# A hybrid attention and 32-expert layer: router on unscaled rows, first and last experts in another order, down weights in 8 KB pieces, activations transposed by every eighth column

## What is computed

```python
x = x + concat([y_a, y_b]) @ w_o                  # x1
h = rms_norm(x, g_ffn)                            # h2
logits = (h @ w_router + b_router)                # 512 x 32
top_vals, top_idx = top_k(logits, 4);  gates = softmax(top_vals)
# for each expert e, for the rows that chose it (at most 128 at a time):
gu  = xb @ w_gu[e] + b_gu[e]                      # 1024 -> 2048
glu = minimum(gu[:, :1024], 7.0);  lin = clip(gu[:, 1024:], -7.0, 7.0)
act = glu * sigmoid(1.702 * glu) * (lin + 1.0)
y   = (act @ w_down[e] + b_down[e]) * gate        # 1024 -> 1024
out = x + sum of the y of each row's four experts
```

## Time and profile before

| | us |
|---|---|
| median of 3 runs | 1613.7 (1611.57 to 1614.81) |
| the profiled execution | 1612.47 |
| its span, first to last instruction | 1610.7 |
| TensorE busy | 1479.8 (92%) |
| VectorE busy | 1313.3 (82%) |
| ScalarE busy | 1107.4 (69%) |
| GpSimd busy | 298.1 (19%) |
| mean granted TensorE clock | 0.955 of full |

### The profile page before, as it was taken

One profiled execution on the slowest core, in us unless ns is written; L12 is line 12 of the kernel. 1 busy time (PEld: TensorE's weight loads), 2 busy tenths in 40 slices (PEclk: granted clock), 3 DMA queues, 4 the chain that ended last, 5 costly groups with the idle time before them and its releaser, 6 DMA issues.

```text
span 1610.7 us, 18681 instructions
## 1 busy us (share of the span) xinstructions
PE 1479.8 (92%) x7095; PEld 1218.0 (76%) x7098; DVE 1313.3 (82%) x1251; ACT 1107.4 (69%) x1198; POOL 298.1 (19%) x161
## 2 busy tenths in 40 slices
PE   6888758997589999999999999999999999999993
PEld 5776646776467888888888888888888888888882
DVE  4668856544668999999999999999999999999991
ACT  5543354443557787778878878887787788877771
POOL 1634301001201111121112111211121121111101
PEclk9999957998799999999999999999999999999997
DMA  6312011107589999999999999999999999999960
GB/s 190 92 53 63 3 53 40 40 27 284 201 268 335 367 373 355 372 368 371 371 371 372 373 353 372 367 369 373 372 372 366 361 368 367 369 371 367 380 257 14
DMA packets 98204, 448.66 MB, mean 279 GB/s; under 512 B 17328, under 2 KB 18480, under 8 KB 65264
## 3 DMA queue, kind: packets, MB, share of 16 engines
q1 hardware_dynamic: 87264, 428.39, 69.1%
q0 software_dynamic: 9792, 18.90, 4.9%
q10 hardware_dynamic: 1040, 0.00, 0.0%
HBM read 440.95 MB, written 23.07 MB: 288 GB/s over the span
## 4 chain that ended last, share of the span: by engine, by line
PE 82%; DVE 10%; ACT 3%; issue 3%; DMA 1%; POOL 0%; SPq 0%; ACTq 0%; DVEq 0%; POOLq 0%
PE ps L1699 65%; PE ps L1493 2%; PE ps L1500 2%; PE ps L1494 2%; PE ps L1495 2%; PE ps L1709 2%; PE ps L1660 2%; PE ps L1668 2%; DVE work L1223 1%; PE ps L1581 1%; DVE top L1222 1%; DVE rp L1180 1%; DVE ss L1159 1%; DMA out_dram<-ysb 1%; PE ps L1610 1%
## 5 line engine op out<-in xcount | busy, mean ns | idle before, releaser
L640 DVE TENSOR_TENSOR whl<-wraw,whl 128x2048 fp32r<-128x2048 f32 x383 | 863.4, 2287 | 92.9 <-ACT whl L635 84.6
L635 ACT ACTIVATE whl<-wraw 128x2048 fp32r<-128x2048 f32 x384 | 732.5, 1919 | 206.6 <-PE ps L1699 206.6
L1699 PE MATMUL ps<-whl,xT 128*128 128x512 f32 x3072 | 722.7, 393 | 0.8 <-DVE whl L640 0.8
L1699 PEld LDWEIGHTS ps<-whl,xT 128*128 128x128 f32 x3072 | 573.7, 189 | 121.4 <-issue 2.2
L1699 PE MATMUL ps<-whl,aT 128*128 128x512 f32 x1536 | 360.9, 394 | 5.9 <-issue 5.9
L1699 PEld LDWEIGHTS ps<-whl,aT 128*128 128x128 f32 x1536 | 288.9, 190 | 65.3 <-issue 6.1
L808 POOL DMA_INDIRECT out_dram<-ysb,idx x32 | 99.3, 3104 | 461.2 <-ACT ysb L1064 461.2
L799 POOL DMA_INDIRECT xg<-h_rows,idx x32 | 86.5, 2702 | 479.4 <-DVE idx L1395 455.7
L1493 PE MATMUL ps<-W,HT 128*128 128x512 f32 (+1 forms) x184 | 72.2, 392 | 1.7 <-DVE HT L1135 1.7
L1494 PE MATMUL ps<-W,HT 128*128 128x512 f32 (+1 forms) x184 | 70.3, 382 | 0.0
L1495 PE MATMUL ps<-W,HT 128*128 128x512 f32 (+1 forms) x184 | 70.2, 381 | 0.0
(11 more groups left out here) (229 smaller groups left out, 1453.8 us busy)
## 6 DMA issues: line engine op xcount, KB each, us to landing
wraw<-in_w_gu_dram SPq DMA_DIRECT2D x256, 1024.0 KB, 8.1
wraw<-in_w_down_dram SPq DMA_DIRECT2D x128, 1024.0 KB, 7.0
WR<-in_w_in_dram SPq DMA_DIRECT2D x20, 512.0 KB, 3.7
WR<-in_w_o_dram SPq DMA_DIRECT2D x8, 512.0 KB, 3.7
xs<-in_x_dram SPq DMA_DIRECT2D x4, 512.0 KB, 5.9
WR<-in_x_dram SPq DMA_DIRECT2D x4, 512.0 KB, 4.3
out_dram<-WR SPq DMA_DIRECT2D x4, 512.0 KB, 2.6
h_rows<-WR SPq DMA_DIRECT2D x4, 512.0 KB, 2.6
```

The lines of the kernel that those rows point to most:

```text
L635: act.activation(whl[:, n % HL, 0, :], wraw[n % RAW], ACT.Copy).then_inc(chunk_hi, 1)
L640: eng.tensor_tensor(whl[:, n % HL, 1, :], wraw[n % RAW], whl[:, n % HL, 0, :].bitcast(F32), ALU.subtract).then_inc(chunk_lo, 1)
L1699: ins = pe.matmul(bank, a[x_][j], w[:, b, j, 512 * q:512 * q + 512], start=c == NG and j == 0 and n == 0, stop=last and j == nj - 1 and n ...
```

## The change

- **Router.** The gain `g_ffn` is multiplied into the router weights once, at setup (`gfcol`, a second column-wise load of 1,024 numbers). The transposes take x1 instead of h2 (`turn_x1`, two units earlier, `route` one unit earlier), and the root is applied to the 32 logits.
- **One-hot.** idxf, a one-hot `one_t`, `selm` and `selb` are made per row block; the 512-wide `one` is made later, in `spread_gates`.
- **First slots.** The one-hots of experts 0 and 1 are made by VectorE (`first_slots`) instead of ScalarE. The maximum count is made after both indices, and has a semaphore of its own. GpSimd no longer does the split of chunk 1; the first splits are VectorE's, after the gates. The bias products of expert 0 come before the first transposes, the gates' products after them.
- **Expert 0 to 1.** Two chunks of expert 1 (LEAD) are split before the activation of expert 0, and VectorE makes the activation before the rest of the next rows. One dense eviction moves by a chunk.
- **End.** `turn_a(31)` is queued within down(30); it writes where the rows of expert 31 were (`xT`), and down(31) uses the gate/up banks. ScalarE and VectorE have the matching order.
- **Last wait.** SyncE waits for the last scatter at its very end; GpSimd does not in round 0.
- **Down weights.** Partition p takes rows 8p + 2q and 8p + 2q + 1 for chunk q, which is one piece of 8 KB instead of two of 4 KB; the transposes of the activation take every eighth column to match, in all 32 experts.

VectorE, from the last block's logits (`lg`) to the start of the gates: before,

The diff at its core:

```diff
     late = {-5: ["mix_b"], -3: ["mix_norm"], 3: ["mix_a"], 4: ["turn_y"], 13: ["post"],
-            14: ["post_mean"], 15: ["post_norm"], 16: ["turn_h2"], 17: ["route"]}
+            14: ["turn_x1", "post_mean"], 15: ["post_norm"], 16: ["route"]}
...
-            return w_down[0, e].rearrange("(q j p) n -> q p j n", q=ND, j=2)[c - NG]
+            return w_down[0, e].rearrange("(p q j) n -> q p j n", q=ND, j=2)[c - NG]
...
             stream(0)
             more_rounds(sp, stream)
+            sp.wait_ge(scattered, 16 * (T + E))
...
-            pool.wait_ge(chunk_lo, 1)
-            split_lo(pool, 0, 0, 1)
...
-                after(pool, passed_ok, 2 * E * r)
-                pool.wait_ge(scattered, 16 * (T + E * r + E))
+                if not is0(r):
+                    pool.wait_ge(passed_ok, 2 * E * r)
+                    pool.wait_ge(scattered, 16 * (T + E * r + E))
...
+            act.dma_start(gfcol, g_ffn[0].rearrange("(k p) -> p k", p=P), allow_slow_non_contiguous=True) \
+               .then_inc(gfcol_in, 16)
...
-                    dve.tensor_tensor(lg[:, t, :], ps[:, ACC, 0:E], brt, ALU.add).then_inc(logit_ok, 1)
+                    dve.scalar_tensor_tensor(out=lg[:, t, :], in0=ps[:, ACC, 0:E], scalar=tss[:, 2:3], in1=brt,
+                                             op0=ALU.mult, op1=ALU.add).then_inc(logit_ok, 1)
...
+            def first_slots(r, j):
+
+                if j == 0 and is0(r):
+                    dve.wait_ge(routed, 1)
+                elif j == 0:
+                    dve.wait_ge(round_step, r)
+                for t in range(T):
+                    ins = dve.tensor_scalar(oh[:, j, t, :], iota, rank[:, t, j:j + 1], None, ALU.is_equal)
+                ins.then_inc(slots_ok, 1)
...
+                for c in range(LEAD):
+                    split_lo(dve, r, 1, c)
                 lin(r, 0)
+                activate(r, 0)
                 turn_x_lo(r, 1)
-                activate(r, 0)
...
                         ins = pe.transpose(ps[:, TP + b, k * P:(k + 1) * P],
-                                           acts[:, 2, (4 * b + k) * P:(4 * b + k + 1) * P], ident)
+                                           acts[:, 2, :].rearrange("p (m k) -> p k m", k=KD)[:, 4 * b + k, :], ident)
...
             def down(r, e):
-                banks = [ps[:, DN + q, :] for q in range(2)]
-                pe.wait_ge(yrow_ok, T + E * r + e)
+                banks = [ps[:, dn_bank(e) + q, :] for q in range(2)]
+                if e == E - 1:
+                    pe.wait_ge(act_ok, E * r + E)
+                else:
+                    pe.wait_ge(yrow_ok, T + E * r + e)
...
+                    if e == E - 2 and c == NG + 1:
+                        turn_a(r, E - 1)
```

More of the change, by code:

```diff
@@ L302, in build @@
         sinr = place("sinr", [P, T, ROT], F32)
+        selm = place("selm", [P, T, E], F32, offset=at["free"])
+        one_t = place("one_t", [P, TOPE, E], F32, offset=at["free"] + 512)
         lamv = place("lamv", [P, 4, HD], F32)
@@ L319, in build @@
         lg = place("lg", [P, T, E], F32)
+        selb = place("selb", [P, T, E], BF16)
         top8 = place("top8", [P, T, 8], F32)
@@ L1004, in slots @@
             def slots(r, j):
-                if is0(r) and j == 0:
-                    act.wait_ge(routed, 1)
-                elif j == 0:
-                    act.wait_ge(round_step, r)
-                after(act, gate_ps, E * r + j - 1 if j or not is0(r) else 0)
+                after(act, gate_ps, E * r + j - 1)
                 after(act, slots_ok, E * r + j)
@@ L1087, in act_round @@
                 for i in range(1, E):
-                    for c in range(NG):
+                    for c in range(LEAD if i == 1 else 0, NG):
                         split_hi(act, r, i, c)
@@ L1106, in act_round @@
                     split_hi(act, r, i - 1, NCH - 1)
-                for c in range(NG, NCH):
-                    split_hi(act, r, E - 1, c)
+                split_hi(act, r, E - 1, NG)
+                split_hi(act, r, E - 1, NG + 1)
+                turn_a_hi(r, E - 1)
+                split_hi(act, r, E - 1, NG + 2)
                 y_rows(r, E - 2)
-                turn_a_hi(r, E - 1)
+                split_hi(act, r, E - 1, NG + 3)
                 y_rows(r, E - 1)
@@ L1328, in _ @@
                                              op1=ALU.mult).then_inc(h2_ok, 1)
-                elif kind == "turn_h2":
+                elif kind == "turn_x1":
                     g = TURN[st]
@@ L1481, in dve_round @@
                     split_lo(dve, r, i - 1, NCH - 1)
-                for c in range(NG, NCH):
-                    split_lo(dve, r, E - 1, c)
+                split_lo(dve, r, E - 1, NG)
+                split_lo(dve, r, E - 1, NG + 1)
                 turn_a_lo(r, E - 1)
+                split_lo(dve, r, E - 1, NG + 2)
+                split_lo(dve, r, E - 1, NG + 3)
             dve_round(0)
@@ L1600, in _ @@
                         ins.then_inc(acc_ps, 1)
-                elif kind == "turn_h2":
+                elif kind == "turn_x1":
                     t = st[1]
-                    pe.wait_ge(h2_ok, t + 1)
+                    pe.wait_ge(x1_ok, t + 1)
                     for j in range(2):
-                        turn(TURN[st] + j, [h2[:, (4 * j + k) * P:(4 * j + k + 1) * P] for k in range(4)])
+                        turn(TURN[st] + j, [x1[:, (4 * j + k) * P:(4 * j + k + 1) * P] for k in range(4)])
                 elif kind == "route":
                     t = st[1]
-                    wait_turns(pe, through(("turn_h2", t)))
+                    wait_turns(pe, through(("turn_x1", t)))
+                    pe.wait_ge(wrt_ok, 1)
                     for k in range(KD):
-                        ins = pe.matmul(ps[:, ACC, 0:E], h2T[:, k, :], wrt[:, k, :], start=(k == 0),
+                        ins = pe.matmul(ps[:, ACC, 0:E], x1T[:, k, :], wrt[:, k, :], start=(k == 0),
                                         stop=(k == KD - 1))
                     ins.then_inc(logit_ps, 1)
-            pe.wait_ge(picked, 1)
+            pe.wait_ge(picked, T)
             for t in range(T):
@@ L1710, in gate_up @@
                 ins.then_inc(bias_mm, 1)
+            def gate_up(r, i):
+                banks = [ps[:, GU + q, :] for q in range(4)]
+                if i:
+                    gate_up_bias(r, i)
                 pe.wait_ge(xT_lo, 2 * E * r + 2 * i + 2)
@@ L1729, in down @@
                     k = 2 * (c - NG)
-                    chunk_products(r, e, c, [[aT[:, a, k + j, :] for j in range(2)] for a in range(2)], banks)
+                    chunk_products(r, e, c, [[a_of(e)[:, a, k + j, :] for j in range(2)] for a in range(2)], banks)
+                    if e == E - 2 and c == NG + 1:
+                        turn_a(r, E - 1)
             def pe_round(r):
```

113 lines of the change are left out of this document (67 added, 46 removed).

## The result

| | before | after | ratio |
|---|---|---|---|
| median of 4 runs each, same chip | 1612.72 us (1611.57 to 1614.81) | 1587.32 us (1585.2 to 1593.24) | 0.9847, 95% interval 0.9818 to 0.9876 |
| profiled execution (its span) | 1612.5 us (1610.7) | 1587.36 us (1585.6) | |

What follows compares the result with a forecast made beforehand. TensorE alone was taken to bound the expert stream (500 to 1550 us), with gains only outside it. 12.6 + 3.6 + 11.9 - 2.0 - 0 = 26.1 us gave 1587.6 us against the median; forecast range 1580 to 1595 (chance 0.52).

Steps and rivals of the forecast that it cites:

- Part 1: Last block's x1 to first expert product: new router and one-hot order gains 12.6 us, bounds 8 and 15.
- Late next if the gather is quick: Before the first product: VectorE, through gates and first split at 409.2, one us before needed, would be the next limit.
- Part 2: Expert 0 to 1: 2.5 us by order plus 1.1 by clock, 3.6 us gained, bounds 2 and 5.
- Part 3: The end: last products 7.1 us earlier, moved scatter wait 4.8 us, 11.9 us gained, bounds 6 and 16.
- last product near 1558 (1584 less 26): Sign at the end of the kernel: when the last product would come, in us.
- Part 4: Added gain-column packets at the start and VectorE steps in the three earlier row blocks: -2.0 us, bounds 0 and -4.
- half of 3.3: Three earlier row blocks: four more VectorE steps (1.1 us) in each, of which half the total was charged.
- Part 5: Strided activation transposes, 256 blocks in the expert stream: taken as 0 us, called the weakest choice.
- (a): Strided activation transposes: the stride costs 10 to 26 us, 1601 to 1610 for most of it; chance 0.27.
- (c): Strided activation loads go at VectorE's 1.99 ns an element: 37 us lost, slower at 1624; chance 0.08.
- Rival (b): Front gain given back by late gather, late VectorE gates or longer expert 2 pause; end only 7.1: 1598; chance 0.13.
- (d): Expert stream between 500 and 1550 us: already at 100%, so its pace stays; part of the forecast, no chance given.

Runs made afterwards that it cites:

- The part alone gave 2.4 in the pause: Kernel before with only the order between experts 0 and 1 changed (two chunks split ahead, activation earlier, one dense eviction a chunk later): 1610.03 us, one run.
- The part alone gave 6.7 us in its trace: Kernel before with only GpSimd's last scatter wait given to SyncE: 1606.17 us (10 runs), ratio 0.9963.
- the old order: Kernel after with the x1 transposes and router step of the first three row blocks back at their old places: 1588.86 us (4 runs), ratio 0.986.
- the one built for it: Kernel after with every x load strided too, for its transposes and the gate/up products (output not the layer's): 1645.16 us, one run.

## Why the prediction was right, and where only its sum was

| term | forecast | measured in the profiled executions |
|---|---|---|
| 1 routing to first product | 12.6 | 13.0 to the first product, -1.5 in the first chunk: 11.5 |
| 2 expert 0 to 1 | 2.5 + 1.1 | 1.6 + 1.9 |
| 2 pause before expert 2 | 0 | 0.9 |
| 3 last products | 7.1 | 6.9 |
| 3 wait moved | 4.8 | 6.8 |
| 4 what is added | -2.0 | -4.4, of which 1.1 before the first x1 |
| 5 stride | 0 | 0 |
| sum | 26.1 | 25.2 |

That the sum met the median within 0.3 us is luck: single terms are off by up to 2.4 us, and the four runs spread over 8. That parts 1 to 3 gave what they did is not luck: their mechanisms were right but for one step of the last wait.

**Part 1, right in mechanism, 1.1 over.** Counted from the last x1, the index came at 11.4 us where the steps gave 10.1. The router products took 2.52 us, not 1.8, because the clock fell to half in the middle of them (granted 0.98 up to 399.7, then 0.50). They, the copy of the index (0.49 us, not 0.15) and VectorE's rank step (0.84 us; 0.24 before) are the difference; the last two ran while GpSimd cleared the gather buffers. The gather took 4.6 us from its start to the transposes, where 4.8 were counted. "Late next if the gather is quick" was VectorE's first split, and that is what happened: the chain goes through it at 412.79 to 414.9, some 0.4 us late (transposes to first product 3.76 us instead of the 3.4 that were worked out). The charge of 1.8 us for half clock was 1.5.

**Part 2, the sum right, its two pieces each off.** The working forgot the four bias products between the activation and expert 1's first product. At full clock they are 0.9 us; in the kernel after they took 1.94. The part alone gave 2.4 in the pause (forecast 2.5) and 2.5 in the chunk behind it (forecast 1.1). The clock makes the difference: in the kernel after it is granted at 0.51 from 447.4 to 450.8, over the bias products and into the chunk, in the part alone at 1.00 from 452 to 462. Why it stayed up there no run shows. The 0.9 us before expert 2 are this execution's: with the same order the whole stretch took 45.9 to 51.7 us over five traces.

**Part 3, the end order, right**: wait 1.21 where 1.6 was worked out, last products 6.9 us earlier relative to the stream. **The wait, mis-sized by 2 us.** The step was "6.3 - 1.55": GpSimd would walk on when its scatter instruction ends, 1.55 us after it starts. By the records it didn't wait for that: the load of the count starts 0.2 us ahead of the scatter (1574.7 against 1574.94). So 6.3 + 0.2 = 6.5 us go instead of 4.8, and some 0.2 more because the walk took 5.0 us instead of 5.2. The landing was sized rightly: before, the load of the count starts at 1599.6, just where 6.3 us from 1593.26 put it. What the prediction calls a walk of 11.1 us is 5.2 us of walk and 5.63 of DRAIN, the same in both kernels. SyncE's wait ended at 1581.5, 4 us before the end of the span, so it sets nothing here. The part alone gave 6.7 us in its trace. One of the signs was also reckoned wrongly: "last product near 1558 (1584 less 26)" takes off the gains of the end, which 1584 already has; by the sum's own terms it is 1591.3 less 21.3, 1570, and it came at 1573.0.

**Part 4, mis-sized.** The step "half of 3.3" for twelve VectorE steps was wrong: with the steps away from the blocks, all 3.4 us came back, so together they cost in full, all 3.1 us of them and a little more. By blocks, against the kernel with the steps deferred (44.2, 43.0 and 27.2 us from x1 to x1), it is 1.3, 1.0 and 1.3 us in the kernel with only the fourth eviction moved (45.6, 44.0 and 28.5), but 0.4, 3.2 and -0.1 in the kernel after (44.6, 46.2 and 27.1), with about the same total. That a step ahead of a maximum has no cover, since VectorE and TensorE wait for each other at every attention head, fits this and the timeline, but it is argued: with the old order the same steps cost 6.0 us, more than they last. The gain column was 0.6 in the forecast (with 1.65 for the steps that makes 2.25, not 2.0); the first block's x1 is 1.1 us later than before, but executions differ by 3 us there, so nothing is shown of it. Only with this 1.1 does the term reach -4.4, outside its bound of -4.

**Part 5, the value right, the reasoning wrong.** I chose zero against my own reading, "loads set that pace and a slower one shows in full". They don't: the recorded load was longer than a block's 109 ns already in the earlier trace rows, so records overlap, and another 47 ns changed nothing. The reason given for zero, that these loads are slower than bf16 ones anyway, has no support either. Rivals (a) and (c) priced the right mechanism at the wrong place: strided loads cost 20 ns a product where the load engine feeds 512-column products of these words, and on such products, not on the transposes, a kernel that ends slower than before is to be had: the one built for it took 1645 us. The Trainium skill, "Advanced Engine Details and Errata", section "Memory Cachelines", says that a new 16-byte line at each access is penalised. The loads agree with it, 141 to 188 and 188 to 330 ns; on the time of this kernel the measurement decides, and it is zero.

**Rival (b)** did not hold in the time. The early gather was in time, VectorE with its gates and first split late by only some 0.4 us, and the pause before expert 2 did not stretch in the profiled execution. With a slower transfer it does: in the trace of the kernel with the deferred steps, 11.76 us and 51.7 us for the stretch. **(d)** held: the distance from expert to expert is the same.

## What to carry to other kernels

A row of a load that is longer than the pitch of what it feeds says nothing about who sets the pace; look at the load engine's idle time (108.8 us down to 1.3 where the loads came to set the pace), and change only the load. Put small steps of one engine where its timeline shows it waiting: the same twelve steps cost 3.4 us or more between attention heads and nothing that shows ahead of the last x1. After a large sum comes out right, still undo its smaller terms one by one: here two of them, the added steps and a pause that I had left at zero, were worth a further 7.4 us in the trace, and 8 by the medians. And where a wait is to be moved, look at the rows of the engine's queue behind it: here they split the 11.1 us into walk and DRAIN, and show when the walk starts.

## What the runs showed of the hardware that I had not expected

- A load of 128x128 fp32 words at a step of eight is recorded at 188 to 192 ns instead of 140, with no effect on a transpose's 109 ns; for a 128x128 load of the rounded words that a product uses, 330 instead of 188 ns, and then 247 ns a product instead of 227.
- The 8 KB pieces (56,506 packets between 500 and 1500 us instead of 70,850) changed neither the DMA engines' share of 0.96 nor the 368 GB/s.
- The accumulating 512 KB write of the third dense row block took 7.5 to 12.2 us from trace to trace in the kernels with the new order, and it sets the pause before expert 2 where ScalarE's next eviction waits for it.
- Three unexecuted rounds are walked by GpSimd in 5.0 to 5.2 us, and the DRAIN behind them takes 5.63. By the records the walk starts 0.2 us ahead of the scatter that is issued before it, not at its end 1.55 us later, and a wait on that scatter ends at the landing time that the DMA view shows (6.3 and 6.6 us from its start).
